# One memory block in runs of columns, turned by VectorE; VectorE's waits put behind the weight remainders

## The reference

```python
mkv = (rms_norm(mem, mem_norm_g) @ w_mem_kv).reshape(bsz, mlen, 2, MEM_HEADS, MEM_HEAD_DIM)
mem_k = rms_norm(mkv[:, :, 0], mem_k_norm_g)
mem_v = mkv[:, :, 1]
h = x
h = h + even_layer(h, ...)   # DeltaNet (8 heads), convolution module (31 taps), attention into mem
h = h + odd_layer(h, ...)    # stick-breaking attention (16 heads), attention into mem
```

## Time and profile before

| what | value |
|---|---|
| time, median of 3 runs | 1313.81 us (1313.45 to 1314.37) |
| time of the profiled execution | 1314.93 us |
| its span in the profile | 1313.2 us |
| busy: PE, DVE, ACT, POOL | 1305.3, 988.5, 747.6, 90.0 us |
| DMA read and written | 250.57 MB, 20.05 MB |

### The profile page before, as it was taken

How to read it: one execution, slowest core, us unless ns; L and a number is a source line. 1 busy time by engine, 2 the same in 40 slices (tenths; PEclk the granted TensorE clock), 3 DMA queues, 4 the chain that set the end, 5 groups by cost and what they waited for, 6 DMA issues and landing times.

```text
span 1313.2 us, 17465 instructions
## 1 busy us (share of the span) xinstructions
PE 1305.3 (99%) x6317; PEld 1097.7 (84%) x6317; DVE 988.5 (75%) x1548; ACT 747.6 (57%) x1173; POOL 90.0 (7%) x91
## 2 busy tenths in 40 slices
PE   9999999999999999999999999999999999999998
PEld 8898889988888888788888888888888888888887
DVE  5468588898988898887667477797788788667663
ACT  5556643576445645586346447748657568555341
POOL 2000200103000100100001020020110200000000
PEclk9999999999999999999999999999999999999999
DMA  8675565765965996685668665765765766978552
GB/s 298 212 210 179 156 198 159 192 209 166 268 179 179 314 299 204 206 252 175 202 204 260 208 191 152 244 194 165 235 198 166 234 193 191 278 216 227 194 193 80
DMA packets 177807, 271.79 MB, mean 207 GB/s; under 512 B 38160, under 2 KB 59577, under 8 KB 177721
## 3 DMA queue, kind: packets, MB, share of 16 engines
q1 hardware_dynamic: 175001, 265.95, 66.5%
q10 hardware_dynamic: 2720, 4.72, 1.1%
HBM read 250.57 MB, written 20.05 MB: 206 GB/s over the span
## 4 chain that ended last, share of the span: by engine, by line
PE 95%; DVE 2%; DMA 2%; ACT 1%; SPq 0%; issue 0%; POOL 0%; ACTq 0%; POOLq 0%
PE job L1983 55%; PE job L1993 27%; PE job L1980 2%; DMA raw<-in_ev_w_in_dram 2%; PE job L1990 1%; PE mixer L2205 1%; PE mixer L2193 1%; DVE wlo L1457 1%; PE mixer L2115 1%; PE mixer L2004 1%; DVE cvr L1724 1%; PE mixer L2215 1%; PE mixer L2223 1%; PE mixer L2095 1%; PE mixer L2128 1%
## 5 line engine op out<-in xcount | busy, mean ns | idle before, releaser
L1983 PE MATMUL job<-whi,xhi 128*128 128x512 f32 x1628 | 647.7, 398 | 0.0
L1983 PE MATMUL job<-whi,xlo 128*128 128x512 f32 x1628 | 634.5, 390 | 0.0
L1457 DVE TENSOR_TENSOR wlo<-raw,whi 128x1024 fp32r<-128x1024 f32 x431 | 527.2, 1242 | 81.5 <-ACT whi L1088 80.3
L1088 ACT ACTIVATE whi<-raw 128x1024 fp32r<-128x1024 f32 x431 | 444.5, 1055 | 215.6 <-PE job L1993 179.7
L1993 PE MATMUL job<-wlo,xhi 128*128 128x512 f32 x1628 | 435.5, 389 | 0.0
L1993 PEld LDWEIGHTS job<-wlo,xhi 128*128 128x128 f32 x1628 | 305.6, 188 | 64.2
L1983 PEld LDWEIGHTS job<-whi,xhi 128*128 128x128 f32 x1628 | 305.9, 188 | 61.4
L1983 PEld LDWEIGHTS job<-whi,xlo 128*128 128x128 f32 x1628 | 306.0, 188 | 61.1
L1724 DVE SCALAR_TENSOR_TENSOR cvr<-cvr,vt 128x255 f32<-128x255 f32 (+14 forms) x240 | 97.9, 465 | 0.0
L1121 ACT ACTIVATE proj<-job,rstd 128x512 f32<-128x512 f32 x74 | 46.6, 683 | 62.2 <-PE job L1993 42.9
L1490 DVE TENSOR_TENSOR hid<-hid,job 128x512 f32<-128x512 f32 x46 | 29.5, 682 | 42.6 <-PE job L1993 39.4
(11 more groups left out here) (307 smaller groups left out, 970.0 us busy)
## 6 DMA issues: line engine op xcount, KB each, us to landing
raw<-in_od_w_in_dram SPq DMA_DIRECT2D x160, 512.0 KB, 4.2
raw<-in_ev_w_in_dram SPq DMA_DIRECT2D x143, 512.0 KB, 4.5
raw<-in_ev_w_out_dram SPq DMA_DIRECT2D x48, 512.0 KB, 5.5
raw<-in_od_w_out_dram SPq DMA_DIRECT2D x48, 512.0 KB, 5.3
raw<-in_w_mem_kv_dram SPq DMA_DIRECT2D x32, 512.0 KB, 4.8
proj<-turned_blocks SPq DMA_DIRECT2D x68, 128.0 KB, 5.0
turned_blocks<-proj SPq DMA_DIRECT2D x9, 512.0 KB, 4.9
turned_blocks<-mix SPq DMA_DIRECT2D x7, 512.0 KB, 4.3
```

The source lines that it names most:

```text
L1088: act(whi[:, c % RING, :, :], raw[:, c % RAWS, :, :], ACT.Copy).then_inc(s_hi, 1)
L1457: vec.tensor_tensor(wlo[:, c % RING, :, :], raw[:, c % RAWS, :, :], whi[:, c % RING, :, :].bitcast(F32), ALU.subtract).then_inc(s_lo, 1)
L1983: mm(pj[j % 2][n][:, :], x[:, s, cols], h, start=first, stop=False)
```

## The change

1. **mem's layout.** mem is loaded by 16 DMAs in place of 4: partition group q (32 partitions) gets runs of 128 columns. A tile of the left operand is every fourth column of 512, so that VectorE's transpose of 32x32 blocks makes two tiles in one instruction (step mt, eight of them, 128x512, the source read at a step of four). TensorE's transposes of mem go. xhi and xlo are then made from SBUF. The rows of w_mem_kv within a chunk, and mem_norm_g, are dealt out by fours to match: a chunk's load reads rows 4p + 2 half and the next one; mem_norm_g is loaded by four DMAs of 4 x 128 numbers with a step of four between numbers.
2. **mem's squares** are eight sums of 512 columns, and VectorE gathers the four partition groups with sixteen small copies and a reduction.
3. **Order.** The VectorE halves of dnV, dnG, rstd, mqs and mks that wait for another engine are steps of their own (dnW, dnM, rsv, mqm, mqr, mkm, mkr), listed in SECOND and sorted with k = 10, behind rest of the same chunk. d6's tail is a step d6f, a chunk later.
4. **Shares and places.** CONV_SHARE from 0.31 to 0.29, a share for mt, xload every two chunks and one chunk earlier, ar to mao two chunks in place of three.

```diff
+SECOND = ("dnM", "dnW", "rsv", "mqm", "mqr", "mkm", "mkr")
+CONV_SHARE = 0.29
...
-            placed.append((int(pos), k, len(placed), step))
+            placed.append((int(pos), 10 if step[0] in SECOND else k, len(placed), step))
...
-        s += [(("dnB", h0 + 3), 1), (("dnV", g), 2), (("dnR", g), 2.5)]
-        s += [(("dnG", h), 1) for h in range(h0, h0 + 4)]
+        s += [(("dnB", h0 + 3), 1), (("dnV", g), 0), (("dnW", g), 2), (("dnR", g), 2.5)]
+        for h in range(h0, h0 + 4):
+            s += [(("dnG", h), 0), (("dnM", h), 1)]
...
-        last = [(("d6", g), 1)] + [(("gate", h), .25) for h in range(h0, h0 + 4)]
+        last = [(("d6", g), 1), (("d6f", g), 0)] + [(("gate", h), .25) for h in range(h0, h0 + 4)]
...
-    stream(3, oa + 2, [(("xload", b), 4) for b in range(4)])
+    stream(3, oa + 1, [(("xload", b), 2) for b in range(4)])
...
-        stream(5, CH0[J_MEM] - 11 + k, [(("xt", F_MEM + k), 0)])
-        stream(5, CH0[J_MEM] - 2 + k, [(("xt", F_MEM + 8 + k), 0)])
+        for half, start in ((0, CH0[J_MEM] - 11 + k), (8, CH0[J_MEM] - 2 + k)):
+            if k % 2 == 0:
+                stream(5, start - 1, [(("mt", (half + k) // 2), 0)])
+            stream(5, start, [(("xt", F_MEM + half + k), 0)])
...
-        return [[(("mas", n), 2), (("mat", n), 0), (("aw", n), 2), (("ar", n), 3), (("mao", 2 * n), .5), (("mao", 2 * n + 1), 0)]
+        return [[(("mas", n), 2), (("mat", n), 0), (("aw", n), 2), (("ar", n), 2), (("mao", 2 * n), 0), (("mao", 2 * n + 1), 0)]
...
-    stream(5, max(CH0[J_MEM] - 6, q + 2), [(("rstd", 1), 0)])
+    stream(5, max(CH0[J_MEM] - 6, q + 2), [(("rstd", 1), 1), (("rsv", 1), 0)])
...
+                if name == "mem":
+                    m, half = divmod(c - CH0[j], 2)
+                    src = w[name][512 * m:512 * m + 512, c0:c0 + 512].rearrange("(p k) n -> p k n", k=4)[:, 2 * half:2 * half + 2]
...
+                if n == 0:
+                    src = src.rearrange("k p -> (k p)").rearrange("(m p r) -> m r p", m=4, r=4)
+                    for m in range(4):
+                        sp.dma_start(dst[4 * m:4 * m + 4, :], src[m], allow_slow_non_contiguous=True).then_inc(s_vrow, 16)
+                    continue
...
-                sc.dma_start(memx[:, :, 512 * b:512 * b + 512],
-                             mem[:, 512 * b:512 * b + 512].rearrange("(t p) d -> p t d", p=128)).then_inc(s_min, 16)
+                for q in range(4):
+                    sc.dma_start(memx[32 * q:32 * q + 32, :, 128 * b:128 * b + 128],
+                                 mem.rearrange("(a i) (m q d) -> m q i a d", i=32, m=4, q=4)[b, q]).then_inc(s_min, 16)
...
+            def do_mt(p):
+                ve.wait_ge(s_min, 256)
+                ve.wait_ge(s_xl, F_OA + 8 if p < 2 else F_MEM + 2 * p - 2)
+                vec.transpose(memt[:, 2 * (p % 2):2 * (p % 2) + 2, :].rearrange("p k s -> p (k s)"),
+                              memx.rearrange("p a (m j r) -> p m r a j", m=4, r=4)[:, p // 2, 2 * (p % 2):2 * (p % 2) + 2]).then_inc(s_jt, 1)
...
-            def do_dnG(h):
+            def do_dnM(h):
                 ve.wait_ge(s_eq, h + 1)
                 v = aq[:, 2 * (h % 4):2 * (h % 4) + 2, :, :].rearrange("p m c n -> p (m c n)")
                 vec.tensor_tensor(v, M[0][:, :], v, ALU.mult).then_inc(s_aq, 1)
...
             def do_xt(n):
-                if F_H <= n < F_H + 12:
+                if F_MEM <= n < F_H + 12:
                     return
```

More of the change, by code:

```diff
@@ L296, in make_plan @@
         p = stream(2, p, [(("ln" + "abo"[i], n - i), 0) for i in range(3) if 0 <= n - i < 8] + [("wait", 1)])
-    stream(4, oa + 1, [(("mqs", i), 1) for i in range(2)])
+    for i in range(2):
+        stream(4, oa + 1 + i, [(("mqs", i), 0), (("mqm", i), 2), (("mqr", i), 0)])
     ks = after(J_MEM) + 1
     for b in range(2):
-        stream(4, ks, [(("mks", b), 0)])
+        stream(4, ks, [(("mks", b), 0), (("mkm", b), 1), (("mkr", b), 0)])
         p = turn_job(6 + b, ks + 2) + 3
@@ L325, in make_plan @@
         stream(5, CH0[J_ODIN] + 4 + (k - 12) // 2, [(("xt", F_H + k), 0)])
-    stream(5, CH0[J_ODIN] + 1, [(("rstd", 2), 0)])
+    stream(5, CH0[J_ODIN] + 1, [(("rstd", 2), 1), (("rsv", 2), 0)])
     stream(6, CH0[J_ODIN] + 4, [(("sbk", 0), 0)])
@@ L337, in make_plan @@
         stream(5, after(J_ODIN + 4 * g + 3) - 1, [(("zb", 4 * g + i), 1) for i in range(4)])
-    p = stream(6, max(p + 1, after(J_ODIN + 17)), [(("mqs", 2), 1), (("mqs", 3), 1)])
+    p = max(p + 1, after(J_ODIN + 17))
+    for i in (2, 3):
+        stream(6, p, [(("mqs", i), 0), (("mqm", i), 2), (("mqr", i), 0)])
+        p += 1
     for e in (8, 9):
@@ L693, in banks @@
             if step == "xt":
-                return [] if F_H <= i < F_H + 12 else [i % 3 if 8 <= i < F_OB else i % 4]
+                return [] if F_MEM <= i < F_H + 12 else [i % 3 if 8 <= i < F_OA else i % 4]
             if step == "mao":
@@ L783, in turned @@
         def turned(n):
-            return n + 1 if n < F_OA else n - F_MEM + 17 if n < F_OB else n - F_H - 12 + 33
+            return n + 1 if n < F_OA else n - F_H - 12 + 17
         def mix_tile(n):
@@ L1135, in do_xt @@
                     return
+                if F_MEM <= n < F_OB:
+                    sc.wait_ge(s_jt, turn_count["mt", (n - F_MEM) // 2])
+                    fill_wait(n)
+                    act(xhi[:, SLOT[n], :], memt[:, n % 4, :], ACT.Copy, scale=xt_gain(n)).then_inc(s_xh, 1)
+                    return
                 sc.wait_ge(s_xp, turned(n))
@@ L1155, in do_rstd @@
                     sc.wait_ge(s_xl, F_H + 8)
+                if src == 1:
+                    for a in range(8):
+                        ins = act(pflat[:, 512 * (a % 4):512 * (a % 4) + 512], memx[:, a, :], ACT.Square, accum_out=msum[:, a:a + 1])
+                        if a == 3:
+                            link(ins)
+                    ins.then_inc(s_ss, 1)
+                    return
                 o = 2048 if src == 0 else 0
-                link(act(pflat[:, 0:2048], (memx if src == 1 else hid)[:, 0, :], ACT.Square, accum_out=ssq[:, src, 0:1]))
-                ins = act(pflat[:, o:o + 2048], (memx if src == 1 else hid)[:, 1, :], ACT.Square, accum_out=ssq[:, src, 1:2])
+                link(act(pflat[:, 0:2048], hid[:, 0, :], ACT.Square, accum_out=ssq[:, src, 0:1]))
+                ins = act(pflat[:, o:o + 2048], hid[:, 1, :], ACT.Square, accum_out=ssq[:, src, 1:2])
                 ins.then_inc(s_ss, 1)
@@ L1346, in squares @@
                 if i == 4:
-                    sc.wait_ge(s_xp, turned(F_MEM + KT - 1))
+                    sc.wait_ge(s_xl, F_OB)
                 unused = reg[:, 3072:4096] if i >= 4 else scr
@@ L1499, in do_first @@
                 ve.wait_ge(s_vt, 1)
+            def do_mt(p):
[3 more added lines that the diff above has]
+                              memx.rearrange("p a (m j r) -> p m r a j", m=4, r=4)[:, p // 2, 2 * (p % 2):2 * (p % 2) + 2]).then_inc(s_jt, 1)
             def do_xt(n):
                 ve.wait_ge(s_xh, n + 1)
+                if F_MEM <= n < F_OB:
+                    vec.scalar_tensor_tensor(out=xlo[:, SLOT[n], :], in0=memt[:, n % 4, :], scalar=xt_gain(n),
+                                             in1=xhi[:, SLOT[n], :].bitcast(F32), op0=ALU.mult, op1=ALU.subtract).then_inc(s_xl, 1)
+                    return
                 if F_H <= n < F_H + 12:
@@ L1518, in do_mf, with do_rsv @@
                                   xhi[:, SLOT[n], :].bitcast(F32), ALU.subtract).then_inc(s_xl, 1)
-            def do_rstd(src):
+            def do_rsv(src):
                 ve.wait_ge(s_ss, src + 1)
+                if src == 1:
+                    for a in range(4):
+                        for b in range(4):
+                            ins = vec.tensor_copy(mquar[32 * a:32 * a + 32, :, b], msum[32 * b:32 * b + 32, a:8:4])
+                    link(ins)
+                    link(vec.tensor_reduce(ssq[:, src, :], mquar[:, :, :], AX.X, ALU.add))
                 vec.tensor_scalar(ssq[:, src, :], ssq[:, src, :], 1.0 / D, EPS, ALU.mult, ALU.add).then_inc(s_ms, 1)
```

57 lines of the change are left out of this document (28 added, 29 removed).

## The result

The changed kernel takes **1334.34 us** (median of four runs, 1329.37 to 1337.56) beside 1314.09 for the kernel before on the same chip: a ratio of 1.015, 95% interval 1.0134 to 1.0166. It is slower, and by more than the range allowed. Its profiled execution took 1329.37 us with a span of 1327.6, so 14.4 us of span more than before are there to be explained; by the medians it is 20.3. In the slower runs the mean granted clock of TensorE was lower (0.992 at 1336.41 and 1337.56, 0.994 at 1332.27, 0.996 at 1329.37): what the profile shows is the mild case.

What follows compares the result with a forecast made beforehand. TensorE was taken as the bound, with other engines' work free unless it waits for them. Terms -4.0 - 0.9 + 3.3 + 5.8 = +4.2 us on 1313.8 gave 1318.0 us, 8-in-10 range 1311.0 to 1323.0.

Steps and rivals of the forecast that it cites:

- the gain's rows at the start: Start: four loads of single numbers on SP ahead of raw chunks 6 to 8 delay TensorE, +3.3 us (0 to 9.5).
- The upper end: Rival at the start: four engines get four times the pieces, 9.5 us in place of 3.3, total 1324.2; chance 0.17.
- Transposes, -4.0: Mem's tiles: 16 pairs of transposes leave TensorE at 0.25 us a pair, -4.0 us with hardly any spread.
- The products: Second DeltaNet half: decay products behind remainders make TensorE wait ahead of dnG7 and delay the inversion, +5.8 us (3.0 to 7.6).
- The channel sum: Mem's stage: TensorE's one wait for GpSimd's sum of the channels goes, -0.9 us (0 to -0.9).
- Sixteen tiny copies ... nothing: Mem's stage, VectorE: the eight squares and sixteen copies for the row sums cost nothing.
- the transposes "hidden": Mem's stage: VectorE's eight transposes, 0.70 us each, 5.6 us in all, are hidden by waits given up and the remainders' lead.
- the fourth rival: Mem's stage: VectorE's transposes at twice the price become the bound, some +2 on the forecast; no chance of its own.
- Seven chunks ahead of job 22's eviction: nothing: Mem's stage: the squares and copies lie seven chunks ahead of job 22's eviction, so they cost nothing.
- mao, xload, ScalarE's issues, nothing: Attention passes and mem's loads: mao a chunk earlier, x every two chunks, ScalarE's 4.8 us more of issues: 0 us.
- neither wait: Rival: VectorE's lead and hidden pieces remove the costs at the start and dnG6, sum -4.9, total 1308.9; chance 0.14.

Runs made afterwards that it cites:

- experiment 3: The kernel before with only mem_norm_g loaded by four DMAs of 4 x 128 single numbers: 1326.40 us, ratio 1.0089.
- experiment 1: The changed kernel with mem's gain by one load of 512 four-number runs, behind chunks 6 and 7 and the beta columns: 1324.43 us, ratio 1.0073.
- experiment 9: The kernel before with the gain's rows by one load of 2,048 single numbers onto 16 rows: 1323.78 us, ratio 1.0073.
- experiment 2: The changed kernel with dnM out of SECOND, so the products of the decays come ahead of the remainder again: 1328.21 us, ratio 1.0102.
- experiment 5: The changed kernel with the edits of experiment 1 and experiment 2 together: 1316.32 us, ratio 1.0018 to the kernel before.
- experiment 8: The best version: experiment 5 plus planner price 0.41 per transpose and the sixteen copies, sum and mean of mem's squares on GpSimd: 1310.07 us, ratio 0.9972.
- experiment 10: experiment 8 with dnM in SECOND again, so the products of the decays come behind the remainder: 1316.46 us, ratio 1.0016.
- experiment 6: experiment 5 with one copy of the eight sums in place of the sixteen tiny copies on VectorE: 1314.31 us, ratio 1.0003.
- experiment 11: experiment 8 with the planner's price of a transpose left at 0.26, so only the copies are moved: 1314.22 us, ratio 0.9995.
- experiment 4: The kernel before with dnM alone split off and put behind the remainder: 1322.33 us, ratio 1.0057.

## Why the prediction was wrong

**What failed is the size of one term: "I take +3.3 us"** for the gain's rows at the start. The place in the order, the chain (raw chunk, split, xlo, TensorE) and the wait's name were right; the chunk that came late was 6, though, where the prediction followed 8, and TensorE stood ahead of chunk 5. It measured 10.2 us in the changed kernel (10.5 by the second DeltaNet half) and 11.4 alone (experiment 3). The working took the landing of L851's 2,048 pieces, 2.4 us more than a chunk's, and 0.48 us for each issue. But SP's standing at the issues is what cost: 12.01 us for four, against the 0.9 counted for three more. The 0.48 was the issue of L851 itself; the issue behind it stands for 7.02 us in the same trace, and this the prediction did not read. With the load of 16 rows back at its place (1.18 us) the start was as before (experiment 1). The upper end, 9.5, was built from the landing too and was still too low. The spread over four engines, from which the prediction argued for that end (the Trainium skill, "DMA: Bandwidth & Descriptors", section on why a DMA increments its semaphore by 16), explains at most the 2.7 us of experiment 9. The other sentence cited, that a strided last dimension becomes one descriptor per element (the Trainium skill, "DMA: Bandwidth & Descriptors", Rules for kernel authors), bears on the count, and 8.7 us go with the count (experiment 9 against the kernel before). Why SP stands behind such a load stays open.

**Transposes, -4.0**: 4.04 us in the changed kernel (14.31 to 10.27), and 4.05 in each of experiments 1, 2, 5 and 8.

**The products, +5.8 (3.0 to 7.6)**: the mechanism came as written. The size was 3.9 in the changed kernel (10.46 to 14.35), 6.5 alone, 7.5 in experiment 1, 6.4 in the best version. The wait of 3.0 us ahead of dnG7 was 2.9 alone and 2.1 where the convolution steps were replanned. The part behind dnG7 is 2.4 in the changed kernel and in experiment 1; what differs lies at d4x. One part is the clock in the five microseconds behind d4x: 1.00 in the changed kernel, 0.67 to 0.70 in the other three. 5 x (1 - 0.67) is 1.65 us of TensorE's work, a cost that the prediction did not have. In the changed kernel:

```profile
370.00:375.00 5.00, 5.00 (x32) 4.41 (x31) 4.41 (x9) 1.37 (x3) 0.00 (x0) 1.00 1.02 353
```

The other is the landing of the inverse's second store: from inC's issue to inD's it took 4.2 us in the changed kernel (357.00 to 361.20), 4.4 alone, 5.4 in experiment 10 and 6.1 in experiment 1 (346.56 to 352.62). The two parts account for the loss at d4x: 1.5 us in the changed kernel, 3.3 alone, 4.1 in experiment 10, 5.0 in experiment 1. Why the store landed later there was not tried, nor why the clock stayed up in the changed kernel.

**The channel sum, -0.9**: wrong in sign. The wait grew from 0.9 to 2.7 us. The argument let VectorE gain from the waits that it gives up, and left out the copies; and where TensorE is faster it asks for the sum sooner (experiments 6 and 11: 2.7 us). It was shorter than before only in experiments 8 and 10, 0.5 and 0.8, where the last convolution step stands two chunks later.

**"Sixteen tiny copies ... nothing" and the transposes "hidden"**: wrong, and this is what the fourth rival named: VectorE's transposes as the bound. Its price per transpose held (1.55 times as slow, within its "twice"), but its +2 was too small: with the channel sum the stage cost 3.9 us in the changed kernel (10.27 to 14.15) and 4.9 in experiment 5, where the forecast had -0.9. "Seven chunks ahead of job 22's eviction: nothing" looked at who needs the sums, and not at what stands behind the copies on VectorE: the last transpose.

**mao, xload, ScalarE's issues, nothing**: right but for 0.3 us. At 547 and at 925 us the difference is 14.1; in between it is up to 1.7 us more where a mao stands one chunk earlier, and comes back. Some 0.3 us of the end arise near 1218 us, in the second attention pass.

**The sum**: -4.0 + 10.4 + 3.9 + 3.9 = 14.2, and those 0.3. The forecast was +4.2. Of the 10.0 us between them the start's term is 7.1, VectorE's queue in mem's stage 4.8, and the products give back 1.9. The median lies 5 us above the profiled run. The two runs with a mean clock 0.004 lower take 7 and 8 us more; of these 0.004 x 1336 = 5.3 us are TensorE's clock, by an estimate. No trace was kept of them, so where they lose it is open. That waits set off the low clock is read from windows and was not tried by itself.

**The rival on the other side**, neither wait: its sum, 1308.9, is close to what experiment 8 reached, 1310.07, once three causes were mended and not two.

## What to carry to other kernels

A DMA is charged twice, at its issue and at its landing: count the single pieces it breaks into, and ask what is queued behind it on the issuing engine. Read the price of an issue from the row behind it as well as from its own. Before a term is called hidden, add up the whole queue of the engine that hides it over the few chunks ahead of the next hand-over, tiny instructions too, and give the planner the durations of the trace. When the bound engine gets faster in one stage, the waits behind that stage come closer: mend one lateness and look for the next, which it had covered.

## What the runs showed of the hardware

- 2,048 single numbers of 4 bytes from DRAM held SP's queue for 12.01 us in four loads on 4 rows each, and for 10.9 us in one load on 16 rows; the same 8 KB in 16 pieces take 1.18 us and 0.42 for the next. The issue behind the load of many pieces is the one that stands: 8.15 us behind the first 512 single numbers, 9.66 behind 2,048, 7.02 behind the 2,048 pieces of 64 bytes of the beta columns, 5.62 in experiment 1 at the same place. From 20 to 25 us, with the earlier transfers through, the DMA share is 0.11 (the changed kernel) and 0.14 (experiment 9).
- In and behind TensorE's waits of 9.15 and 9.8 us the granted clock was 0.50 to 0.64 over five-microsecond stretches (0.50 is 1.2 GHz), and stretches of 0.67 to 0.76 go with the waits of 2.33 (experiment 4), 2.7 (5), 3.1 (10), 3.2 and 4.0 us (1). Such a wait costs more than its length: in experiment 5 one of 2.7 us moved the chunks by 4.7. Behind those of 2.09, 2.15 and 2.7 us in the changed kernel, and behind the one of 2.9 in experiment 4, the clock stayed at 1.00, so the length alone does not tell.
- VectorE's transpose of 128x512 takes 1.08 us when its source is read at a step of four, 0.70 when it is not. A copy of 32x2 takes VectorE 0.17 us and GpSimd 0.37 (5.89 for sixteen).
